# Sparse attention on parts of the TensorE array: four column strips, two row halves, two column halves

## What is computed

```python
kc = jnp.einsum('bnlgd,lde->bnge', k_cmp[:, blk_idx], w_cmp_k)   # 15 windows of 32 tokens, stride 16
vc = jnp.einsum('bnlgd,lde->bnge', v_cmp[:, blk_idx], w_cmp_v)
...
s = jnp.einsum('bqgrd,bngd->bgrqn', qb, kc) * scale
p_cmp = masked_softmax(s, cmp_end[None, :] <= t[:, None], axis=-1)
o_cmp = jnp.einsum('bgrqn,bngd->bqgrd', p_cmp, vc)
...   # the same with the selected keys (here all of them) and with a sliding window of keys
o = gb[:, :, 0] * o_cmp + gb[:, :, 1] * o_slc + gb[:, :, 2] * o_win
```

## Time and profile before

| | |
|---|---|
| median of three runs | 1660.27 us (1659.91 to 1661.56) |
| span of the profiled execution | 1658.2 us |
| PE busy | 99% |
| DVE busy | 61% |
| ACT busy | 46% |
| DMA engines busy (queue 1) | 61.2% |

### The profile page before, as it was taken

The page is one execution under the profiler, slowest core; times in us unless marked ns, Lnnn a source line. Parts: engine busy times, 40 slices in busy tenths (PEclk is TensorE's granted clock), DMA queues, the critical chain, the costliest instruction groups (busy, mean ns, idle before and its releaser), DMA issues.

```text
span 1658.2 us, 20072 instructions
## 1 busy us (share of the span) xinstructions
PE 1636.7 (99%) x7623; PEld 1351.8 (82%) x7623; DVE 1016.7 (61%) x1217; ACT 765.8 (46%) x887; POOL 0.7 (0%) x5
## 2 busy tenths in 40 slices
PE   9999999999999999999999999999999999999996
PEld 7888887778888888888888888888888888888885
DVE  6557737654998997886555544555545555555564
ACT  7444435555443445344454434444344434444453
POOL 0000000000000000000000000000000000000000
PEclk9999989999999999999999999999999999999998
DMA  9676545454766667876556556655665556555653
GB/s 330 195 265 206 179 149 165 142 172 138 241 191 203 203 177 267 267 257 242 186 181 188 189 192 192 189 184 193 194 188 181 189 192 195 182 189 182 213 191 101
DMA packets 164290, 326.64 MB, mean 197 GB/s; under 512 B 10737, under 2 KB 15985, under 8 KB 163313
## 3 DMA queue, kind: packets, MB, share of 16 engines
q1 hardware_dynamic: 164208, 325.54, 61.2%
HBM read 315.01 MB, written 10.49 MB: 196 GB/s over the span
## 4 chain that ended last, share of the span: by engine, by line
PE 89%; DVE 8%; ACT 1%; issue 1%; DMA 1%; SPq 0%; ACTq 0%; DVEq 0%
PE ps L361 28%; PE ps L363 28%; PE ps L362 28%; DVE sb L344 3%; PE ps L377 2%; DVE sb L1450 1%; PE ps L640 1%; PE ps L684 1%; PE ps L592 1%; ACT sb L337 0%; PE ps L667 0%; DVE sb L1457 0%; DVE sb L1456 0%; DVE sb L1463 0%; DVE sb L1462 0%
## 5 line engine op out<-in xcount | busy, mean ns | idle before, releaser
L344 DVE TENSOR_TENSOR sb<-sb,sb 128x1024 fp32r<-128x1024 f32 x560 | 683.6, 1224 | 512.4 <-ACT sb L337 501.5
L337 ACT ACTIVATE sb<-sb 128x1024 fp32r<-128x1024 f32 x560 | 593.2, 1060 | 764.9 <-PE ps L363 741.0
L361 PE MATMUL ps<-sb,sb 128*128 128x512 f32 x2240 | 878.0, 392 | 1.9 <-DVE sb L344 1.9
L363 PE MATMUL ps<-sb,sb 128*128 128x512 f32 x2240 | 870.6, 389 | 0.0
L362 PE MATMUL ps<-sb,sb 128*128 128x512 f32 x2240 | 870.4, 389 | 0.0
L361 PEld LDWEIGHTS ps<-sb,sb 128*128 128x128 f32 x2240 | 421.7, 188 | 91.5 <-issue 7.6
L363 PEld LDWEIGHTS ps<-sb,sb 128*128 128x128 f32 x2240 | 421.5, 188 | 88.1
L362 PEld LDWEIGHTS ps<-sb,sb 128*128 128x128 f32 x2240 | 421.8, 188 | 84.3
L1575 DVE TENSOR_TENSOR sb<-sb 128x1024 f32<-128x1024 f32 x16 | 19.6, 1225 | 26.4 <-ACT sb L1056 26.4
L392 DVE TENSOR_TENSOR sb<-ps,sb 128x1024 fp32r<-128x1024 f32 x26 | 31.7, 1218 | 1.4 <-ACT sb L383 1.4
L1056 ACT ACTIVATE sb<-ps,sb 128x512 f32<-128x512 f32 x32 | 20.2, 684 | 24.7 <-PE ps L363 24.5
(11 more groups left out here) (225 smaller groups left out, 474.5 us busy)
## 6 DMA issues: line engine op xcount, KB each, us to landing
sb<-in_w_in SPq DMA_DIRECT2D x128, 512.0 KB, 3.8
sb<-in_w_up SPq DMA_DIRECT2D x128, 512.0 KB, 3.7
sb<-in_w_down SPq DMA_DIRECT2D x128, 512.0 KB, 3.6
sb<-in_w_mix SPq DMA_DIRECT2D x64, 512.0 KB, 3.7
sb<-in_w_branch SPq DMA_DIRECT2D x32, 512.0 KB, 5.3
sb<-in_w_out SPq DMA_DIRECT2D x32, 512.0 KB, 3.7
sb<-in_w_pg SPq DMA_DIRECT2D x32, 512.0 KB, 3.7
gate_mem<-sb SPq DMA_DIRECT2D x16, 512.0 KB, 5.0
```

What stands on the lines that cost most here:

```text
L337: act.activation(whi[:, j % RING, :], raw[:, j % RING, :], ACT.Copy).then_inc(hi_done, 1)
L344: eng.tensor_tensor(wlo[:, j % RING, :], raw[:, j % RING, :], whi[:, j % RING, :].bitcast(F32), ALU.subtract).then_inc(lo_done, 1)
L361: pe.matmul(o, xh, w_h, start=first and k == 0, stop=False)
L363: mm = pe.matmul(o, xl, w_h, start=False, stop=last and k == TK - 1)
```

## The change

Compression: the tokens of a window are split into two halves of 16. For each of the 16 residues, the stationary operand is `kv_ct[:, :, b::16]` (2 groups x 16 blocks = 32 columns), and the moving one `w_cmp[:, b:32:16, :]` (both halves, 2 x 128 columns). The 16 matmuls go in turn to four column strips of 32 (four sums in four strips of PSUM, in turn i = 0 to 3). At a new place, A_SEL (6), eight full-array matmuls with a constant 0/1 matrix `cmp_sel` add the strips and the two halves and lay the results out as values `xg` (128 rows, zeros outside a head's 32) and as keys `kc_t`, on both row halves. `cmp_sel` is one more DMA of 256 KB, issued after `w_cmp`; the transposes L607 and L612 go.

Scores: q is transposed twice (once as before, once shifted by 64 columns), so that each head's q stands on both row halves; the keys for the selected part lie on rows 0 to 63 and those for the window on rows 64 to 127. Of two successive matmuls one uses each half, and they write different PSUM banks. The same holds for the compressed scores, with the two token blocks on the two halves; they are split over A_CS and A_CS + 1, and the step that takes their exponential moves from `A_CS + 2` to `A_CS + 3` on ACT and DVE. A_PCT stays at 13.

Values: heads 2r and 2r + 1 are done together at the odd head, in turn on column halves 0 and 1; the compressed part has 128 rows now. Even heads run only `scores(hd + 1)`.

The columns of q and kv in the input projection change places. The core of the diff (left out: the mask of the scores on DVE, which covers the same elements in another layout; the semaphores' names; the order of input columns):

```diff
-A_BAND, A_POOL, A_QTR, A_KTR, A_CS, A_PCT = 2, 4, 7, 8, 9, 13
+A_BAND, A_POOL, A_SEL, A_QTR, A_KTR, A_CS, A_PCT = 2, 4, 6, 7, 8, 9, 13
...
                     sp.dma_start(w_cmp[:, :, :], a["w_cmp"]).then_inc(cmp_in, 16)
+                    sp.dma_start(cmp_sel[:, :, :], a["cmp_sel"]).then_inc(cmp_in, 16)
...
-            o = aux[1][:, C:C + NG * NCMP].rearrange("p (g n) -> p g n", g=NG)
-            for l in range(32):
-                mm = pe.matmul(o, w_cmp[:, l, :], kv_ct[:, :, l:l + 16 * (NCMP - 1) + 1:16],
-                               start=l == 0, stop=l == 31)
+            for b0 in range(0, 16, 4):
+                for i in range(4):
+                    mm = pe.matmul(aux[1][32 * i:32 * i + 32, C:C + 2 * P], kv_ct[:, :, b0 + i:S:16],
+                                   w_cmp[:, b0 + i:32:16, :], start=b0 == 0, stop=b0 == 12)
             mm.then_inc(sg["cmp_sum"], 1)
+            until(A_SEL)
+            pe.wait_ge(sg["cmp_sb"], 1)
+            for g in range(NG):
+                for i in range(2):
+                    pe.matmul(aux[1][:, g * DH:(g + 1) * DH], cmp_sel[:, 2 * g + i, :], cmp_part[:, i, P:P + DH],
+                              start=i == 0, stop=i == 1)
+            for g in range(NG):
+                for i in range(2):
+                    mm = pe.matmul(aux[1][:, P + g * CP:P + (g + 1) * CP], cmp_part[:, i, 0:P],
+                                   cmp_sel[:, 2 * g + i, 0:CP], start=i == 0, stop=i == 1)
+            mm.then_inc(sg["xg_sum"], 1)
...
             until(A_KTR)
+                    mm = pe.transpose(aux[1][:, o:o + P], z[:, tt, KV0 + (2 + g) * P:KV0 + (3 + g) * P], ident[:, :])
+            mm.then_inc(sg["k_tr"], 1)
+            pe.wait_ge(sg["xg_sb"], 1)
+            q_pairs(Q0 + 4 * P - DH, aux[1][:, S:2 * S])
+            pe.wait_ge(sg["q_sb"], 1)
+            for k in range(4):
+                mm = q_pairs(Q0 + k * P - DH, aux[0][:, k * S:(k + 1) * S])
+            mm.then_inc(sg["q_tr"], 1)
...
+            def cmp_scores(rr):
+                for g in range(NG):
+                    for tt in range(TT):
+                        o = tt * C + (g * R + rr) * CP
+                        mm = pe.matmul(aux[1][:, o:o + CP],
+                                       q_t[tt * DH:(tt + 1) * DH, q_block(2 * rr + g, tt), tt * P:(tt + 1) * P],
+                                       kc_t[tt * DH:(tt + 1) * DH, g, :], start=True, stop=True)
...
                 for tt in (1, 0):
                     for i in range(2):
-                        mm = pe.matmul(aux[0][:, o:o + n], q_t[lo:lo + DH, hd // 2, tt * P:(tt + 1) * P],
-                                       k_t[lo:lo + DH, i, 0:n], start=True, stop=True)
+                        o = i * C + (0 if tt else S)
+                        mm = pe.matmul(aux[0][:, o:o + n],
+                                       q_t[i * DH:(i + 1) * DH, q_block(hd, i), tt * P:(tt + 1) * P],
+                                       k_t[i * DH:(i + 1) * DH, hd % 2, 0:n], start=True, stop=True)
...
+            until(A_CS)
+            pe.wait_ge(sg["k_sb"], 1)
+            pe.wait_ge(sg["q_sb"], 2)
+            cmp_scores(0)
+            cmp_scores(1)
+            until(A_CS + 1)
+            cmp_scores(2)
+            cmp_scores(3).then_inc(sg["cs_done"], 1)
             scores(0)
...
+                if hd % 2 == 0:
+                    continue
...
                 for i in range(2):
                     for kt in range(2):
-                        pe.matmul(o[:, kt * P:S], z[:, kt, v0:v0 + DH], b, start=first, stop=False)
+                        for g in range(NG):
+                            v0 = KV0 + (4 + i) * P + g * DH
+                            pe.matmul(o[g][:, kt * P:S], z[:, kt, v0:v0 + DH],
+                                      prob_t[:, g, (3 * i + 2 * kt) * P:(3 * i + 2 + kt) * P],
+                                      start=i == 0 and kt == 0, stop=False)
-                pe.matmul(o, xg[rr * CP:(rr + 1) * CP, g, DH:P], pc_t[rr * CP:(rr + 1) * CP, g, :, :],
-                          start=False, stop=True).then_inc(sg["pv_done"], 1)
+                for g in range(NG):
+                    mm = pe.matmul(o[g], xg[:, 2 * rr + g, :], pc_t[:, g, :, :], start=False, stop=True)
+                mm.then_inc(sg["pv_done"], 1)
...
-            until(A_CS + 2)
+            until(A_CS + 3)
             act.wait_ge(sg["cs_sub"], 1)
```

More of the change, by code:

```diff
@@ L599, in _ @@
             for k in range(4):
-                for tt in range(TT):
-                    mm = pe.transpose(aux[0][:, k * S + tt * P:k * S + (tt + 1) * P],
-                                      z[:, tt, Q0 + k * P:Q0 + (k + 1) * P], ident[:, :])
+                mm = q_pairs(Q0 + k * P, aux[0][:, k * S:(k + 1) * S])
             mm.then_inc(sg["q_tr"], 1)
-            pe.wait_ge(sg["cmp_sb"], 1)
-            for g in range(NG):
-                mm = pe.transpose(aux[1][:, g * P:(g + 1) * P], kvc[:, g, :, :], ident[:, :])
@@ L608, in _ @@
-            mm.then_inc(sg["xg_tr"], 1)
             until(A_KTR)
[L610 to L619, removed]
@@ L620, in _ @@
-            until(A_CS)
-            pe.wait_ge(sg["kc_sb"], 1)
             for g in range(NG):
                 for tt in range(TT):
[L625 to L630, removed]
+                    o = C + g * S + tt * P
@@ L1259, in _ @@
             v.wait_ge(sg["pool_lo"], 1)
[L1260 to L1273, removed]
+            for i in range(2):
+                k = aux[1][:, C + i * P:C + i * P + DH].rearrange("p (o e) -> p o e", o=1)
+                v.tensor_copy(cmp_part[:, i, 0:P].rearrange("p (o e) -> p o e", o=2), k.to_broadcast([P, 2, DH]))
+            v.tensor_copy(cmp_part[:, :, P:P + DH],
+                          aux[1][:, C:C + 2 * P].rearrange("p (a e) -> p a e", a=2)[:, :, DH:P]).then_inc(sg["cmp_sb"], 1)
+            until(A_SEL)
+            v.wait_ge(sg["xg_sum"], 1)
+            v.wait_ge(sg["xg_zero"], 1)
+            for rr in range(R):
+                rows = slice(rr * CP, (rr + 1) * CP)
+                v.tensor_copy(xg[rows, 2 * rr:2 * rr + 2, :].rearrange("p g e -> p (g e)"), aux[1][rows, 0:NG * DH])
+            v.tensor_copy(kc_t[:, :, :].rearrange("p g n -> p (g n)"), aux[1][:, P:P + NG * CP]).then_inc(sg["xg_sb"], 1)
+            until(A_CS + 1)
             v.wait_ge(sg["cs_done"], 1)
             v.wait_ge(mask_in, 32)
-            sc = aux[1][:, :].rearrange("p (g x) -> p g x", g=NG)[:, :, 0:TT * R * CP]\
-                .rearrange("p g (t r n) -> p t g r n", t=TT, r=R)
+            sc = aux[1][:, :].rearrange("p (t x) -> p t x", t=TT)[:, :, 0:NH * CP]\
+                .rearrange("p t (h n) -> p t h n", h=NH)
             def bc_mask(which, tt):
@@ L1326, in _ @@
                 v.wait_ge(sg["sc_done"], hd + 1)
[L1327 to L1331, removed]
+                both = aux[0][:, :].rearrange("p (i k) -> p i k", i=2)
+                s1, s0 = both[:, :, 0:S], both[:, :, S:S + P]
+                for i in range(2):
+                    edge = both[:, i, P:3 * P].rearrange("p (b k) -> p b k", b=2)
+                    link(v.tensor_tensor(edge, edge, tri[:, :].rearrange("p (o k) -> p o k", o=1).to_broadcast([P, 2, P]),
+                                         ALU.add))
                 v.tensor_reduce(stat[:, hd, 0:2], s1, AX_X, ALU.max, negate=True)
@@ L1652, in compressed_mask, with block_sums @@
     return np.ascontiguousarray(both.transpose(2, 0, 1, 3).astype(np.float32))
+def block_sums():
+    sel = np.zeros((4, NG, 16, NG, 2, R, CP), np.float32)
+    for g in range(NG):
+        for half in range(2):
+            for n in range(NCMP):
+                sel[:, g, n + half, g, half, :, n] = 1.0
+    return np.ascontiguousarray(sel.reshape(P, 2 * NG, P))
 def kernel(x, p, g_mix, w_in, w_cmp_k, w_cmp_v, s5_a_re, s5_a_im, s5_log_dt, s5_b_re, s5_b_im,
@@ L1686 @@
     head_order = np.arange(NH * DH).reshape(NG, R, DH).transpose(1, 0, 2).ravel()
-    pair_order = np.arange(2 * NG * DH).reshape(2, NG, DH).transpose(1, 0, 2).ravel()
-    order = np.concatenate([Q0 + head_order, KV0 + pair_order, np.arange(KV0 + 2 * P, ZS)])
+    kinds = NH * DH + np.arange(6 * NG * DH).reshape(6, NG, DH)
+    order = np.concatenate([kinds[[0, 1]].transpose(1, 0, 2).ravel(), kinds[[2, 4]].transpose(1, 0, 2).ravel(),
+                            kinds[3].ravel(), kinds[5].ravel(), head_order, np.arange(NG0, ZS)])
     w_in = np.asarray(w_in)[0]
```

78 lines of the change are left out of this document (43 added, 35 removed).

## The result

The changed kernel takes 1638.34 us (median of four runs, 1638.13 to 1638.66) against 1660.35 us before (1659.91 to 1661.56): a ratio of 0.9867, 95% interval 0.9855 to 0.9879. The forecast was 1638. The span of the profiled execution went from 1658.2 to 1636.4 us.

The account below looks back on a forecast made before the run. PE's own work was taken to bound the kernel. Its time beyond dense products was to fall from 46.2 to 24.1 us, 22.1 less: span 1658.2 to 1636.1, plus 2.1 for the median, 1638; range 1633.5 to 1644.5.

Parts of the forecast that it names:

- compression on strips: At L592: 8 passes of 256 columns on each strip, with switch, skew and way out, 2.1 us instead of 10.4.
- compressed scores and scores(0), after: At A_CS and A_CS + 1: row halves work side by side and the clock stays up, 3.1 us instead of 7.6.
- an even head; heads 1, 3, 5; head 7: PE's time per head: scores alone 1.05 us; scores and two heads' values 2.95; head 7 2.1; together 15.2 instead of 28.2.
- wait at A_PCT: PE waits 1.2 us at A_PCT, as a 6.5 us chain behind gate tile 11's split has two tiles, 5.45 us.
- ACT's copies of q done ahead of A_CS: ACT's 1280 more copied columns end before PE reaches A_CS, with a margin of 0.7 us, so no cost.
- PE's work is the time: In the changed stretch each microsecond off PE's own work comes off the time, until another engine is late.
- Side by side: Strips and halves of the array run at once, each at its own full rate, also with 256 columns and column halves.
- the rival of a shared port: Passes of 256 columns on array parts share a port: compression, values, scores, A_CS together +19 us, 1657; chance 0.04.
- Strict order: Rival: passes start in program order over all array parts, at compression, scores, values and A_CS; +4.3 us, 1642; chance 0.07.
- the clock's part: Share of the saving from lost clock falls: dense products behind compression 1.7 us and compressed scores 2.3, together 4.0.
- That narrow passes make the clock fall: Passes of 30 or 32 columns, one after another, preceded both falls to 0.50, behind the compression and L627.
- the slower rival: Half-array blocks make the clock fall behind each of eight heads, two existing falls kept: 1667 us; chance 0.03.

## Why the prediction was right

Each step against its measurement, PE's time beyond the dense products:

| step | forecast, us | measured, us |
|---|---|---|
| compression on strips | 2.1 | 2.1 |
| sums at A_SEL | 1.9 | 1.8 |
| transposes, more than before | 0.6 | 0.6 |
| compressed scores and scores(0), after | 3.1 | 3.2 |
| an even head; heads 1, 3, 5; head 7 | 1.05; 2.95; 2.1 | 1.05; 2.94; 2.08 |
| wait at A_PCT | 1.2 | 1.2 |
| ACT's copies of q done ahead of A_CS | 0.7 | some 0.7 |
| less in all, first dense product to the one behind head 7 | 22.1 | 22.1 |
| time | 1638 | 1638.34 |

- **PE's work is the time.** That followed from the list of waits, not from the 99%: it has no wait of PE between the first dense product and 390 us. The prediction read the list too narrowly, though. Besides the 2.2 us of the earlier trace rows it holds 4.1 us more, 1.9 of them on DVE at the very start, and so not "all in the state-space part". It did no harm, since none of these waits lies in the part that changed; but it makes the fall of the busy time (21.7) a poor measure of the work, which fell by some 23 us, as the forecast had it (22.1 and the wait of 1.2).
- **Side by side.** The forecast took the fourfold rate from the earlier trace rows and the two halves from the seam in the earlier trace rows, and carried both to 256 columns and to column halves that no row showed. The four strips of 256 columns in 1.96 us and the head alone on its half show that the carry was sound; the rival of a shared port is refuted by them.
- **Strict order** is refuted: with the parts in turn it would have cost 4.3 us, and part by part far more than the 5.5 measured. The Trainium skill's page "TensorE: Matmul & The Clock Gate" (Part 3, The mechanism) has matmuls start and end in program order; the rival takes this for the passes, each of which stands in the trace as a matmul. These runs disagree: four strips start within 0.02 us of each other when fed in turn, ahead of the first strip's second pass (0.27 later), and part by part a pass of L715 starts at 278.36, ahead of one of L711 at 278.57 that was issued before it.
- **The wait at A_PCT** was forecast from one row's start and a count of tiles, and the kernel without it gives back 1.2 to 1.4 us, 1.2 of them at the place itself.
- **The size of the clock's part was wrong, the sum right.** I put it at 4.0 us, the dense products behind each block. The kernel with the narrow runs broken shows 5.4, or nearly 6 without the estimated price of the breaks. The step that failed is the statement that the clock's share lies behind the blocks: part of L592's 8.62 and of L640's 1.95 in the earlier trace rows was spent at 0.50 as well. The passes of L592 alone, ahead of the fall and in it:

```profile
211.00:215.50 4.50, 4.50 (x43) 4.50 (x42) 1.00 0.13 46
216.00:218.80 2.80, 2.80 (x15) 2.80 (x14) 0.50 0.00 0
```

  A pass starts every 0.112 us in the first stretch and every 0.213 in the second. Fifteen such passes cost 1.5 us, L640's in the second fall 0.8, and the products behind the two 1.7 and 2.3, as forecast: 6.3 together. Since the sum took the blocks at their measured length, the mistake moved some 2 us from one heading to another and did not touch the total.
- **That narrow passes make the clock fall** was taken from what stood before each fall. Adding them brought a fall back, adding wide ones at the same pace did not, and breaking them up took both away. Half-array blocks, on which the slower rival rested, do not do it, neither 6.9 us of them in one piece nor those of the heads.
- The expected spread of outcomes left out that the kernel before is itself uneven: its runs on the other chips lie from 1658.3 to 1663.0, those of the changed kernel within 0.7 us. Where the falls of the clock are gone, the spread is gone too, but for one run (1656.86).

The fastest kernel of the study is the changed one with the exponential at A_CS + 2: 1637.04 us beside 1638.44.

## What to carry to other kernels

Where PE has no waits, small matmuls are worth their passes: put them on different strips or halves, in turn, and read the price of a pass and of the switch from the blocks that are there. A long block of narrow passes can cost time behind it too (here 1.7 and 2.3 us) and be slower in its own last part: look at the granted clock in and behind each, and if it falls, break the block up with dense work before rewriting it. When a step is moved by a tile, count the tiles left to whoever needs its result.

## What was not expected of the hardware

- The order of issue matters for parts of the array: the compression costs 1.96 us in turn and 4.70 strip by strip. In the three blocks that show it (the strips, the column halves, the row halves of L627) the next part starts when four passes of the part before it are left.
- Weight loads with a step of 16 elements cost nothing that shows: eight such passes deep on four strips take 8 x 0.216 us and the ends, and 0.216 is also what a pass of 256 columns of L715 takes, whose weights are read without a step.
- A clock at 0.50 came with PE busy without a gap. Two loads of 64 passes, issued at the same pace of one in 0.112 us, led to 0.50 with 30 moving columns (from 5.0 us into the load) and stayed at 1.00 with 128.
